# Output stage: y turned by transfers on the SP queue, loads of y and gates from ScalarE's queue, y's halves double-buffered

## The reference

```python
def rms_norm(x, g):
    xf = x.astype(jnp.float32)
    y = xf * lax.rsqrt(jnp.mean(xf * xf, axis=-1, keepdims=True) + EPS)
    return (y * g.astype(jnp.float32)).astype(x.dtype)
...
def blocked_attention(q, k, v):
    ...
    def one_block(qblk):
        s = jnp.einsum('bkgqd,bksd->bkgqs', qblk, k).astype(jnp.float32) * scale
        p = jax.nn.softmax(s, axis=-1).astype(v.dtype)
        return jnp.einsum('bkgqs,bksd->bkgqd', p, v)
...
def reference(x, norm_in, w_in, a_q_norm, a_k_norm, b_cq_norm, b_ckv_norm,
              w_uq, w_ukv, b_q_norm, b_k_norm, w_out):
    ...
        xn = rms_norm(h, norm_in[l])
        proj = jnp.einsum('bsd,dn->bsn', xn, w_in[l])
        a_q, a_k, a_v, a_g, b_cq, b_ckv, b_kr, b_g = jnp.split(proj, _SPLITS, axis=-1)
        ...
        y_a = blocked_attention(q, k, v)
        ...
        y_b = blocked_attention(qb, kb, vb)

        y = jnp.concatenate([y_a * jax.nn.silu(a_g), y_b * jax.nn.silu(b_g)], axis=-1)
        h = h + jnp.einsum('bsm,md->bsd', y, w_out[l])
    return h
```

## Time and profile before

| what | us |
|---|---|
| median of 3 runs (1712.44 to 1714.27) | 1714.13 |
| the profiled execution's own time | 1717.09 |
| span of its profile | 1715.3 |
| busy in the span: PE / DVE / ACT / POOL | 1598.0 / 1179.4 / 1128.7 / 565.4 |
| output stage: first transfers issued | 1503.26 |
| first product of the stage | 1519.33 |
| last residual begins | 1711.51 |

### The profile page before, as it was taken

The page is one execution under the profiler, slowest core; times in us unless marked ns, Lnnn a source line. Parts: engine busy times, 40 slices in busy tenths (PEclk is TensorE's granted clock), DMA queues, the critical chain, the costliest instruction groups (busy, mean ns, idle before and its releaser), DMA issues. The chain is left out here.

```text
span 1715.3 us, 39468 instructions
## 1 busy us (share of the span) xinstructions
PE 1598.0 (93%) x14224; PEld 939.9 (55%) x14224; DVE 1179.4 (69%) x1648; ACT 1128.7 (66%) x1458; POOL 565.4 (33%) x478
## 2 busy tenths in 40 slices
PE   5899999999997499999999999999999999969998
PEld 3455555555554146556665566556655665634444
DVE  6555445446445498899889988899889988543332
ACT  8454454454553188888888888888888888743322
POOL 0100000000000056566656666566656666600000
PEclk9999999999999599999999999999999999979999
DMA  8113213213302723233333243223322333045563
GB/s 303 61 41 100 70 37 90 80 35 89 84 23 73 177 93 79 63 77 72 81 69 80 61 93 77 61 58 93 77 61 64 86 77 85 15 153 174 169 184 110
DMA packets 242080, 153.15 MB, mean 89 GB/s; under 512 B 63984, under 2 KB 225264, under 8 KB 242032
## 3 DMA queue, kind: packets, MB, share of 16 engines
q1 hardware_dynamic: 241552, 152.33, 33.1%
q10 hardware_dynamic: 480, 0.20, 0.0%
HBM read 109.85 MB, written 40.92 MB: 88 GB/s over the span
## 5 line engine op out<-in xcount | busy, mean ns | idle before, releaser
L952 POOL TENSOR_TENSOR p_pl<-p_p,p_ph 128x512 f16<-128x512 f32 x384 | 502.3, 1315 | 829.1 <-ACT p_ph L988 770.6
L1003 DVE TENSOR_REDUCE p_part<-p_mx 128x2 f32<-128x1024 f32 x384 | 468.4, 1220 | 86.8 <-PE p_mx L1079 68.6
L979 ACT ACTIVATE p_p<-p_st 128x1024 f32<-128x1024 f32 x384 | 391.3, 1019 | 122.9 <-PE p_st L1111 64.9
L622 PE MATMUL p_ring<-p_w_hi,p_xT 128*128 128x512 f16 (+3 forms) x1536 | 392.0, 341 | 14.3 <-DVE p_w_lo L505 9.7
L988 ACT ACTIVATE p_ph<-p_p 128x1024 f16<-128x1024 f32 x336 | 355.6, 1058 | 19.7 <-ACT p_p L979 2.9
L1031 DVE TENSOR_TENSOR p_pl<-p_p,p_ph 128x512 f16<-128x512 f32 x384 | 325.1, 847 | 9.3 <-ACT p_ph L988 8.5
L622 PE MATMUL p_ring<-p_w_lo,p_xT 128*128 128x512 f16 (+3 forms) x768 | 261.5, 341 | 0.0
L622 PEld LDWEIGHTS p_ring<-p_w_hi,p_xT 128*128 128x128 f16 x1536 | 151.6, 99 | 138.7 <-issue 18.5
L1143 PE MATMUL p_acc<-p_vas,p_ph 128*128 128x129 f16 x2048 | 207.9, 221 | 0.0
L1144 PE MATMUL p_acc<-p_vas,p_pl 128*128 128x65 f16 x2048 | 201.0, 193 | 0.0
L1143 PEld LDWEIGHTS p_acc<-p_vas,p_ph 128*128 128x128 f16 x2048 | 180.7, 97 | 36.4 <-issue 14.3
(11 more groups left out here) (133 smaller groups left out, 2131.7 us busy)
## 6 DMA issues: line engine op xcount, KB each, us to landing
p_vbs<-scratch_vb SPq DMA_DIRECT2D x16, 1028.0 KB, 6.3
p_xin<-in_x SPq DMA_DIRECT2D x16, 512.0 KB, 3.9
scratch_g<-p_g SPq DMA_DIRECT2D x16, 512.0 KB, 3.6
p_kb<-scratch_kb SPq DMA_DIRECT2D x32, 256.0 KB, 5.3
p_gt<-scratch_g SPq DMA_DIRECT2D x16, 512.0 KB, 5.0
p_xr<-in_x SPq DMA_DIRECT2D x16, 512.0 KB, 4.4
out<-p_res SPq DMA_DIRECT2D x16, 512.0 KB, 3.0
early<-in_w_in SPq DMA_DIRECT2D x6, 1024.0 KB, 7.0
```

Source lines behind the costliest of these rows:

```text
L622: last = pe.matmul(ring_t[:, 0:w], a, b, start=(k == 0 and m == 0), stop=(k == len(steps) - 1 and m == len(terms) - 1))
L952: pool.tensor_tensor(pl[:, s % NP, 1, :], p32[:, s % N32, QB:], ph[:, s % NP, 1, :], ALU.subtract).then_inc(s_lop, 1)
L979: act.activation(p32[:, s % N32, :], st[:, s % 2, :, :].rearrange("p a b -> p (a b)"), ACT.Exp, scale=scale).then_inc(s_exp, 1)
L1003: dve.tensor_reduce(part[:, e // MPAIRS % 3, 2 * c:2 * c + 2], mx[:, :, :], AX, ALU.max).then_inc(s_red, 1)
```

## The change

y is no longer turned on TensorE. For each tile the SP queue issues two transposing transfers, from `yh` and from `yl` in SBUF straight into `yT` (`turn` on SP), each raising a semaphore of its own per slot (`s_yt`, `s_ytl`). The unit matrix, the PSUM tiles `tp`, TensorE's `turn` and ScalarE's copies out of PSUM are gone. `yh` and `yl` have two slots. The loads of y and gates for tile t+2 are issued by ScalarE right after the `yh` of tile t; only those of the first two tiles stay on SP. SP's 16 tiles are written out instead of being looped over: in each it turns tile t+1, then stores tile t and loads x for t+2.

```diff
--- before.py
+++ after.py
@@ -1186,17 +1186,14 @@
         sg = sb("sg", [P, 2, D])
         xr = sb("xr", [P, 2, D])
         yg = sb("yg", [P, 2, D])
-        yh = sb("yh", [P, D], F16)
-        yl = sb("yl", [P, D], F16)
+        yh = sb("yh", [P, 2, D], F16)
+        yl = sb("yl", [P, 2, D], F16)
         yT = sb("yT", [P, 2, 2, KT, P], F16)
         res = sb("res", [P, 2, D])
-        eye = sb("eye", [P, P], F16)
-        tp = [ps(f"tp{s}", [P, KT, P], F16) for s in range(2)]
         po = [[ps(f"po{b}{c}", [P, 512]) for c in range(2)] for b in range(2)]
 
         s_whi = sem("w_hi")
         s_wlo = sem("w_lo")
-        s_eye = sem("eye_ready")
         s_y = [sem("y_loaded0"), sem("y_loaded1")]
         s_g = [sem("g_loaded0"), sem("g_loaded1")]
         s_x = [sem("x_loaded0"), sem("x_loaded1")]
@@ -1204,8 +1201,8 @@
         s_yg = sem("y_gated")
         s_yh = sem("y_hi")
         s_yl = sem("y_lo")
-        s_tp = sem("yT_in_psum")
-        s_yt = sem("yT_in_sbuf")
+        s_yt = [sem("yT_hi_turned0"), sem("yT_hi_turned1")]
+        s_ytl = [sem("yT_lo_turned0"), sem("yT_lo_turned1")]
         s_po = sem("out_in_psum")
         s_res = sem("residual_added")
         s_out = [sem("out_stored0"), sem("out_stored1")]
@@ -1223,41 +1220,45 @@
             for h in range(2):
                 body(TILES - 2 + h, h, PAIRS - 1, False, True)
 
+        def load_yg(eng, t, h):
+
+            for g in range(GA):
+                eng.dma_start(ya[:, h, g * 4:g * 4 + 4, :], YA[g].rearrange("h t p d -> t p h d")[t]).then_inc(s_y[h], 16)
+            eng.dma_start(yb[:, h], YB.rearrange("h t p d -> t p h d")[t]).then_inc(s_y[h], 16)
+            eng.dma_start(gt[:, h, :], G[t]).then_inc(s_g[h], 16)
+
         block = ctx.enter_context(nc.Block())
 
         @block.sync
         def _(sp):
-            def load_yg(t, h):
-                for g in range(GA):
-                    sp.dma_start(ya[:, h, g * 4:g * 4 + 4, :], YA[g].rearrange("h t p d -> t p h d")[t]).then_inc(s_y[h], 16)
-                sp.dma_start(yb[:, h], YB.rearrange("h t p d -> t p h d")[t]).then_inc(s_y[h], 16)
-                sp.dma_start(gt[:, h, :], G[t]).then_inc(s_g[h], 16)
-
             for t in range(2):
-                load_yg(t, t)
+                load_yg(sp, t, t)
             for t in range(2):
                 sp.dma_start(xr[:, t, :], xt[t]).then_inc(s_x[t], 16)
 
+            def turn(t, h, free):
+
+                sp.wait_ge(s_yh, t + 1)
+                if free:
+                    sp.wait_ge(s_po, t * 2 - 2)
+                sp.dma_start_transpose(yT[:, h, 0], yh[:, h, :]).then_inc(s_yt[h], 16)
+                sp.wait_ge(s_yl, t + 1)
+                sp.dma_start_transpose(yT[:, h, 1], yl[:, h, :]).then_inc(s_ytl[h], 16)
+
+            turn(0, 0, False)
+
             def tile(t, h, i, first, last):
-                if not last:
-
-                    sp.wait_ge(s_yg, t * 2 + 2)
-                    load_yg(t + 2, h)
+                if not (last and h == 1):
+                    turn(t + 1, 1 - h, not (first and h == 0))
                 sp.wait_ge(s_res, t * 2 + 2)
                 sp.dma_start(ot[t], res[:, h, :]).then_inc(s_out[h], 16)
                 if not last:
                     sp.dma_start(xr[:, h, :], xt[t + 2]).then_inc(s_x[h], 16)
 
-            loop(sp, tile)
+            for t in range(TILES):
+                tile(t, t % 2, t // 2, t < 2, t >= TILES - 2)
             for h in range(2):
                 sp.wait_ge(s_out[h], PAIRS * 16)
-
-        @block.gpsimd
-        def _(pool):
-            pool.memset(eye[:, :], 0.0).then_inc(s_eye, 1)
-            pool.wait_ge(s_eye, 1)
-            pool.affine_select(out=eye[:, :], in_=eye[:, :], compare_op=ALU.not_equal, fill=1.0,
-                               base=0, pattern=[[-1, P]], channel_multiplier=1).then_inc(s_eye, 1)
 
         @block.scalar
         def _(act):
@@ -1279,19 +1280,15 @@
             def tile(t, h, i, first, last):
 
                 act.wait_ge(s_yg, t * 2 + 2)
-                if not (first and h == 0):
-                    act.wait_ge(s_tp, t * 2)
-                act.activation(yh[:, :], yg[:, h, :], ACT.Copy).then_inc(s_yh, 1)
+                if not first:
+                    act.wait_ge(s_yt[h], i * 16)
+                act.activation(yh[:, h, :], yg[:, h, :], ACT.Copy).then_inc(s_yh, 1)
+                if not last:
+                    load_yg(act, t + 2, h)
                 if first and h == 0:
                     split_hi(1)
                 if not (last and h == 1):
                     silu(t + 1, 1 - h, i if h == 0 else i + 1, first and h == 0)
-                for s in range(2):
-                    act.wait_ge(s_tp, t * 2 + s + 1)
-                    if not first:
-
-                        act.wait_ge(s_po, t * 2 - 2)
-                    act.activation(yT[:, h, s], tp[s][:, :, :], ACT.Copy).then_inc(s_yt, 1)
 
             loop(act, tile)
 
@@ -1330,9 +1327,9 @@
 
             def tile(t, h, i, first, last):
                 dve.wait_ge(s_yh, t + 1)
-                if not (first and h == 0):
-                    dve.wait_ge(s_tp, t * 2)
-                dve.tensor_tensor(yl[:, :], yg[:, h, :], yh[:, :], ALU.subtract).then_inc(s_yl, 1)
+                if not first:
+                    dve.wait_ge(s_ytl[h], i * 16)
+                dve.tensor_tensor(yl[:, h, :], yg[:, h, :], yh[:, h, :], ALU.subtract).then_inc(s_yl, 1)
                 if first and h == 0:
                     split_lo(1)
                 if not (last and h == 1):
@@ -1345,17 +1342,9 @@
 
         @block.tensor
         def _(pe):
-            def turn(t, first):
-                for s, src in enumerate((yh, yl)):
-                    pe.wait_ge(s_yh if s == 0 else s_yl, t + 1)
-                    if not first:
-                        pe.wait_ge(s_yt, t * 2 - 1 + s)
-                    for k in range(KT):
-                        last = pe.transpose(tp[s][:, k, :], src[:, k * P:(k + 1) * P], eye[:, :])
-                    last.then_inc(s_tp, 1)
-
             def tile(t, h, i, first, last):
-                pe.wait_ge(s_yt, t * 2 + 2)
+                pe.wait_ge(s_yt[h], i * 16 + 16)
+                pe.wait_ge(s_ytl[h], i * 16 + 16)
                 for c in range(2):
                     cols = slice(c * 512, (c + 1) * 512)
                     if not first:
@@ -1368,11 +1357,7 @@
                             mm = pe.matmul(po[h][c][:, :], yT[:, h, s, k, :], w[:, k, cols],
                                            start=(k == 0 and m == 0), stop=(k == KT - 1 and m == 2))
                     mm.then_inc(s_po, 1)
-                    if c == 0 and not (last and h == 1):
-                        turn(t + 1, False)
-
-            pe.wait_ge(s_eye, 2)
-            turn(0, True)
+
             loop(pe, tile)
```

## The result

The changed kernel takes 1704.66 us (median of 7, 1698.39 to 1707.61) against 1713.61 us (median of 7, 1712.44 to 1714.64): 0.994 of the time before, interval 0.9921 to 0.9958. It is faster by 9 us where 23 were forecast. The profiled execution took 1705.23 us, its span is 1703.4.

What follows compares the result with a forecast made beforehand. Bound: a ring of waits over SP's queue, 12.03 us a tile, with TensorE's 11.27 close. Start 1518.2 + tile 0 12.64 + 15 x 10.5 + tail 3.8 = span 1692.1, median 1691; range 1686 to 1701, 8 in 10 1686 to 1755.

Steps and rivals of the forecast that it cites:

- TensorE's transposes go: Output stage, TensorE: tiles 1 to 15 lose 15 x 0.89 = 13.4 us of transposes between products.
- The ring is cut: Output stage: loads of y and gates leave SP's queue, ending a 12.03 us a tile chain of waits through late gates.
- The price of a turned half: DMA queues, output stage: a half turned by transfer costs 1.2 to 1.9 us, as 1024 pieces of 256 bytes.
- Rival C: Output stage: queues become the bound above 2.6 us a half, slower than before, 1728 to 1943 us; chance 0.25.
- Is there room for it?: Output stage: queues loaded 9.2 to 10.6 us a tile, halves land at 8 to 9.5, needed at 10.4; tile taken as 10.5.
- Start: Start of the output stage: first halves land in 3.0 to 4.4 us, first product at 1518.2, 1.1 us sooner.
- Rival B: Output stage: halves cost 2.1 to 2.5 us or full queues delay them, 11.1 to 11.8 a tile, 1700 to 1711; chance 0.10.
- Sum: Whole kernel: 1518.2 + 12.64 + 15 x 10.5 + 3.8 = 1692.1 us span, 23.2 less than 1715.3; median 1691.

Runs made afterwards that it cites:

- The turn ahead of store and x load: Changed kernel with the turned halves of tile t+2 issued on SP ahead of the store of t and the x load of t+2: 1696.32 us.
- the turn alone: Changed kernel with its loads of y and gates back on SP's queue: 1711.07 us, 0.9981 of the kernel before.
- the held loads: Changed kernel with first x loads behind tile 0's turn and tile 2's loads waiting on ScalarE for tile 0's low half: 1696.13 us.
- the joined run: Changed kernel with tile 2's loads held for tile 0, turns ahead of store and x load, first x loads behind tile 1's turn: 1693.89 us.

## Why the prediction was right in part and missed the size

*TensorE's transposes go.* Right. 768 products at 0.216 us are 165.9; with the slower first ones, TensorE does the stage in 167.5 us where nothing stops it.

*The ring is cut.* Right (the idle time of TensorE that it names is 10.5 us by its own numbers, not 10.7; nothing hangs on it), and shown alone by the run that moves only the loads. The forecast that the loads would not be late next holds: 6.3 us of waits for gates in the stage, and 3.2 of them after the first product.

*The price of a turned half.* Right in size, by an estimate. In the 31.1 us from 1584.5 to 1615.6, three tiles of the changed kernel, the queues show

```profile
q1 hardware_dynamic: 7200, 4.72, 58.0%
q10 hardware_dynamic: 5147, 3.06, 38.9%
```

that is 482 us of queue time in all. Less 1152 pieces of 4 KB at 0.161 us and 4763 small pieces of loads at 0.029 (the prediction's costs, from the kernel before), 159 us are left for six halves, 26.5 each, 1.65 us on each of 16 queues, inside the 1.2 to 1.9 of the forecast. The number of pieces is right as well: 7200 less 768 of store and x, by six, is 1072, near the 1024 pieces of 256 bytes that I took. Rival C falls with that: a half of eight squares lands in 3.1 us where nothing stands ahead of it.

The Trainium skill's 1309 ns for a square by transfer ("VectorE: DVE Perf Modes", "The three transpose paths"), taken for each of eight squares in a row, would make 10.5 us (an estimate), and falls too. The Trainium skill's other page ("Advanced Engine Details and Errata", "X-Bar Transpose (TRN2)"), by which such transfers are as fast as plain ones, is nearer. Even so a half of 256 KB lands in 3.1 us where a store of 512 KB takes 3.0 in the kernel before, and the 1.65 us a queue are over twice the 0.7 us estimated by that page.

*"Is there room for it?"* Failed by a little. From the first product to the last it took 174.0 us instead of 12.64 + 157.5, 3.9 more: 0.6 in tile 0, whose first products ran at a granted clock of 0.50 until 1530, and 3.3 in the 15 tiles behind it, which took 10.72 us each instead of 10.5. The capacity was right (96.9% of 31.1 us, by three, are 10.0 us a tile, inside 9.2 to 10.6); the latency was put at 8 to 9.5 us after TensorE's end of a tile and measured 10.1. That sum is the landing of x, 5.7 us, and two halves at 1.2 to 1.9; the issues of the halves stand in it at nothing, and they hold SP for 1.7 and 2.4 us. With 0.3 us to spare instead of 1 to 2, some halves come late. The turn ahead of store and x load shows that the place in the queue decides; since it shortens landing and hold together, how much of the lateness is the hold itself stays open. The forecast asked whether a turn behind the store fits, and not why it should stand behind.

*"Start".* This is the step that failed most. It took the landing of a store or an x load (3.0 and 4.4 us) for the landing of the first halves, which was 11.1 us; the first product was forecast at 1518.2 and came at 1525.54, 7.3 us of the 11.3 us by which the span missed. A first product after 1520 was one of the prediction's own signs of being wrong. The earlier trace rows are rows of a middle tile, in which one queue serves. At the start, ScalarE's queue issues 1 MB for tile 2 at the very moment yh begins, and the small pieces of the half share 16 engines with it. The runs tell the parts apart: with tile 2's loads kept off the second queue the halves land in 3.2 to 3.5 us, with the x loads ahead (the turn alone) as without them (the held loads), and 7.2 and 7.3 us come back. How the loads slow a half so much more than its own 1.65 us stays open: the window from 1515 to 1525 shows the queues more than fully busy at only 150 GB/s, so pieces took longer there; what they waited for no run shows.

*Rival B.* Its range, 1700 to 1711 us, holds the measured 1704.66, and one of its grounds, that the loads on ScalarE's queue share the engines with the halves, is what the start shows. But it put a price of 11.1 to 11.8 us on every tile, and a tile without a late half took TensorE's own 10.4. That its range holds the number is luck.

*Sum.* 7.3 for the start and 3.9 from the first product on are together 11.2 of the 11.3 us between the span forecast, 1692.1, and 1703.4. The median misses its forecast by 2.4 us more, 13.7: the execution that the sum was set against lay 3.0 us over its median, the one profiled after the change 0.6. With both places mended 1688.52 us are reached, 2.4 below the forecast. That does not confirm the sum to the microsecond, as the reordered start brings the first product at 1516.11, ahead even of the forecast's 1518.2.

## What to carry to other kernels

A transfer that replaces work of an engine has three prices: the bytes on the queues, the hold of the queue that issues it, and the landing, and only the landing decides when its reader starts. Take it from a row with the same neighbours: here 3.1 us with none ahead, 6.7 behind a store and an x load, 11 beside 1 MB of loads on another queue. Put what the bound engine waits for ahead of what nobody waits for in the queue, and look at the first tile by itself; there the buffers that hide a landing are not filled yet.

## What was not expected of the hardware

- A transposing transfer holds the issuing queue for 1.23 us with nothing ahead of it and for up to 4.45 us under load (the high half of tile 2 in the run that joins held loads and turn ahead). A plain one of twice the bytes takes 0.34 to 0.43 in the middle of the changed kernel, but single ones can hold their queue longer too: a load of gates held ScalarE's for 5.95 us at 1528.90 in the joined run.
- A turned half of 256 KB lands in 3.1 us (low) and 3.5 us (high) at the median with nothing ahead of it and in up to 13.0 us beside loads from the other queue.
- An issue on ScalarE's queue leaves at once even where the program has it behind work that the engine has not begun (loads at 1512.30 behind a split that began at 1513.25).
- Behind a wait of 2.6 us TensorE's granted clock was 0.90 in one execution's next 11 us; behind waits of 2.2 and 2.8 us in two other executions 96 products took 20.9 us, the full pace.
